# Two blocks in one launch: splits, sums and output pieces at new places, and the up gate scaled by VectorE

## The chip, the cores and the metric

One Trainium2 chip, one of its cores. The metric is the device time of one launch in microseconds; the kernels are compared by the median of their runs. A profile is one execution taken by the hardware profiler.

## The reference

An input x of 256 tokens by 1024 features goes through two blocks, in float32.

```
first block, for each of 2 layers:
  h = rms_norm(x); proj = h @ w_in                      # 1024 -> q, k, v of two attentions, gates
  y_a = dilated_attention(q, k, v with rope) @ w_proj_a
  y_b = stick_breaking_attention(q, k, v) @ w_proj_b
  x = x + (gate_a * y_a + gate_b * y_b) @ w_out
  h = rms_norm(x); a, b = split(h @ w_up)               # 2 x 2816
  x = x + (silu(causal_conv(a)) * b) @ w_down
x = rms_norm(x)
second block, one layer:
  proj = rms_norm(x) @ w_in                             # qkv, z, b, a, lru_x, lru_gate
  o  = gated_delta_rule(silu(conv(qkv)), ...); gdn = rmsnorm(o) * silu(z)
  hr = rg_lru(conv(lru_x), ...);               lru = hr * gelu(lru_gate)
  x = x + concat(gdn, lru) @ w_out
  u = relu(rmsnorm(x) @ w_ff1); x = x + (u * u) @ w_ff2 # 4096 wide
out = rmsnorm(x)
```

## The kernel before

The activations lie transposed (features on the 128 partitions, 256 tokens along the row), 8 chunks wide. Every weight matrix is cut into slabs of up to 128 x 2048 values (two output tiles of 128 features over 8 chunks; 1024 values where there are 4 chunks). Three slabs are in work at a time (SLOTS = 3): SyncE loads slab n into `raw`, ScalarE rounds it to `w_hi` (fp32r), and VectorE, or GpSimd for the slabs listed in POOL_SLABS, writes the rest `raw - w_hi` to `w_lo`. These are the splits (L1280 on ScalarE, L1776 on VectorE, L2500 on GpSimd). Each product of a chunk is then three matmuls, high by high, high by low and low by high (`main_tile`, L671). SyncE loads slab n + 3 when slab n's low half is written. ScalarE splits slab n + 3 when TensorE has ended slab n. Activations are split in the same way: `xg_hi`/`xg_lo`, and for inner results `hid_high` on ScalarE and `hid_low` on VectorE (L1856). The results of a slab go to PSUM, into three banks in turn (RING = 3), two tiles to a bank for most kinds and one for the kinds that are added to x; a tile may begin when the one three banks earlier has been read.

The order on each engine is written out by hand, one program for each, which wait on semaphores. What stands where in an engine's program is all that sets the order.

Up stages of the first block (L941 for TensorE): slabs of kind "fa" (the convolved half) and "fb" (the other half) alternate, 12 in the first part and 10 in the second, of each layer. For an fa slab VectorE multiplies both tiles by the norm (L2047), ScalarE does the last tap, VectorE the two others, ScalarE splits slab n + 3 and applies silu (L1479), and GpSimd multiplies by the norm (L2555). For an fb slab VectorE multiplies the product by that (L2050), ScalarE writes the high half and then splits slab n + 3, VectorE writes the low half (L2066) and then splits slab n + 3. A pair of slabs is one fa and one fb.

Input stage of the second block (L1152, L2341): 13 slabs. Between tiles and in the middle of tiles TensorE does the small matmuls of the delta rule: `first_x` (L1016) turns the first matrices; for levels 1 to 6 `level_ax`, `level_x` and `turn_x` follow; VectorE answers with `level_mask` (L2245) and `level_add` (L2258), ScalarE with `turned_x`. `key_gain` and `matrix_a` (L2150, L2216) make the matrices that first_x turns. `unit_out` (L2323) is the end of the recurrence: four scans, four products, then four low halves at L2395.

Output stage of the second block: 4 slabs "lru" and 4 slabs "gdn", 4 chunks each; `x_add` (L1792) adds each tile to x. After the lru tile 4 TensorE does `spread_out`, from which VectorE makes the gdn half of the input (L2452) and its low halves. Then `x_stage` (L1803) interleaves x_add, the splits and `x_low` (the low half of the next stage's input), and the up stage of 4096 features begins.

## Time and profile before

| | us |
|---|---|
| median of 3 runs | 1090.31 |
| lowest, highest | 1089.19, 1090.49 |
| the profiled execution | 1091.28 |
| its span | 1089.5 |
| TensorE busy (8400 matmuls) | 1068.8 |
| VectorE busy | 705.4 |
| ScalarE busy | 570.8 |
| GpSimd busy | 353.9 |
| mean granted TensorE clock | 0.996 |

Busy time is the union of an engine's instructions as the profiler shows them; an instruction may be drawn overlapping the next one, above all on TensorE. A row of a timeline gives the start and the length in us, the engine, the line of the kernel, the operation, what is written and read, the shapes, how many like it were merged, and in brackets the idle time ahead of it with what ended it.

### The profile page before, as it was taken

The numbers are of one execution on the slowest core, as the hardware profiler recorded it, in microseconds if no ns is written. First come the engines' busy times: TensorE is split into PE (matmuls) and PEld (weight loads), VectorE is DVE, ScalarE is ACT, GpSimd is POOL, SyncE is SP. The second block draws the span as 40 slices with busy tenths as digits, with TensorE's granted clock in tenths as the row PEclk, the third lists the DMA queues.
The fourth block names the chain that finished last, engine by engine and source line by source line (L and its number), as shares of the span: only waits on it lengthen the run. The fifth ranks groups of instructions, "written<-read, shape, count | busy, mean of one in ns | idle before, by whom it ended". The sixth has DMA issues, their size and how long they took to land.

```text
span 1089.5 us, 20040 instructions
## 1 busy us (share of the span) xinstructions
PE 1068.8 (98%) x8400; PEld 1008.4 (93%) x8400; DVE 705.4 (65%) x1164; ACT 570.8 (52%) x788; POOL 353.9 (32%) x223
## 2 busy tenths in 40 slices
PE   8999999999999999999999999999999999999997
PEld 6999998998899899999999989998989999999996
DVE  4752248767677776222877767777877778667663
ACT  5545466554355544545665544466637856344433
POOL 1386675322023128666642201323200034102020
PEclk9999999999999999999999999999999999999999
DMA  7744454454754665344545475446341156564751
GB/s 251 232 162 138 141 180 156 155 184 149 247 173 141 198 219 182 107 148 152 161 157 185 153 229 194 135 143 212 119 154 41 59 176 204 170 212 136 234 184 39
DMA packets 169689, 180.11 MB, mean 165 GB/s; under 512 B 4224, under 2 KB 166400, under 8 KB 169472
## 3 DMA queue, kind: packets, MB, share of 16 engines
q1 hardware_dynamic: 169600, 178.84, 51.0%
q8 instruction: 66, 1.08, 0.4%
q14 instruction: 23, 0.19, 0.1%
HBM read 177.78 MB, written 1.05 MB: 164 GB/s over the span
## 4 chain that ended last, share of the span: by engine, by line
PE 70%; issue 11%; DVE 10%; ACT 5%; POOL 3%; DMA 1%; SPq 0%; DVEq 0%; POOLq 0%; ACTq 0%
PE psum L669 68%; DVE sb_w_lo L1783 3%; ACT sb_w_hi L1278 2%; POOL sb_scratch L2535 1%; POOL sb_scratch L2555 1%; ACT sb_scratch L1278 1%; DVE sb_scratch L1774 1%; PE psum L865 1%; DVE sb_rs L1832 1%; DVE sb_xg_lo L1774 1%; DVE sb_hid_both L1858 1%; DMA sb_scratch<-in_x 1%; DMA sb_raw<-in_w_ff 1%; DVE psum L1774 0%; ACT sb_xg_hi L1278 0%
## 5 line engine op out<-in xcount | busy, mean ns | idle before, releaser
L669 PE MATMUL psum<-sb_xg_hi,sb_w_hi 128*128 128x256 f32 x1640 | 471.1, 287 | 4.8 <-DVE sb_w_lo L1783 2.8
L669 PE MATMUL psum<-sb_xg_lo,sb_w_hi 128*128 128x256 f32 x1640 | 464.3, 283 | 0.0
L669 PE MATMUL psum<-sb_xg_hi,sb_w_lo 128*128 128x256 f32 x1640 | 464.2, 283 | 0.0
L1278 ACT ACTIVATE sb_w_hi<-sb_raw 128x2048 fp32r<-128x2048 f32 (+4 forms) x184 | 316.0, 1722 | 160.0 <-PE psum L669 97.9
L1783 DVE TENSOR_TENSOR sb_w_lo<-sb_raw,sb_w_hi 128x2048 fp32r<-128x2048 f32 (+3 forms) x150 | 304.8, 2037 | 115.6 <-ACT sb_w_hi L1278 115.5
L669 PEld LDWEIGHTS psum<-sb_xg_hi,sb_w_hi 128*128 128x128 f32 x1640 | 313.9, 191 | 10.7 <-issue 5.8
L669 PEld LDWEIGHTS psum<-sb_xg_lo,sb_w_hi 128*128 128x128 f32 x1640 | 314.2, 192 | 0.4
L669 PEld LDWEIGHTS psum<-sb_xg_hi,sb_w_lo 128*128 128x128 f32 x1640 | 314.0, 191 | 0.2
L669 PE MATMUL psum<-sb_hid_both,sb_w_hi 128*128 128x512 f32 (+1 forms) x912 | 281.7, 369 | 2.3 <-DVE sb_hid_both L1858 1.3
L669 PE MATMUL psum<-sb_hid_both,sb_w_lo 128*128 128x256 f32 x784 | 221.0, 282 | 0.0
L669 PEld LDWEIGHTS psum<-sb_hid_both,sb_w_hi 128*128 128x128 f32 x912 | 164.1, 190 | 36.6 <-issue 3.5
L2506 POOL TENSOR_TENSOR sb_w_lo<-sb_raw,sb_w_hi 128x2048 fp32r<-128x2048 f32 (+1 forms) x34 | 154.9, 4562 | 123.2 <-ACT sb_w_hi L1278 111.1
L669 PEld LDWEIGHTS psum<-sb_hid_both,sb_w_lo 128*128 128x128 f32 x784 | 149.2, 190 | 0.0
L2555 POOL TENSOR_TENSOR sb_scratch<-sb_scratch,sb_rs 128x256 f32<-128x256 f32 x44 | 66.2, 1524 | 242.0 <-ACT sb_scratch L1278 242.0
L1278 ACT ACTIVATE sb_hid_both<-sb_scratch 128x256 fp32r<-128x256 f32 x100 | 40.0, 414 | 96.3 <-DVE sb_scratch L2050 62.7
L1278 ACT ACTIVATE sb_scratch<-sb_scratch,sb_params 128x256 f32<-128x256 f32 x76 | 37.8, 554 | 60.3 <-DVE sb_scratch L2047 60.3
L2583 POOL TENSOR_TENSOR sb_scratch<-sb_scratch 128x256 f32<-128x256 f32 x32 | 23.4, 754 | 125.2 <-DVE sb_scratch L1774 125.2
L1858 DVE TENSOR_TENSOR sb_hid_both<-sb_scratch,sb_hid_both 128x256 fp32r<-128x256 f32 x100 | 51.9, 543 | 4.7 <-ACT sb_hid_both L1278 4.1
L1278 ACT ACTIVATE sb_scratch<-psum 128x256 f32<-128x256 f32 (+3 forms) x58 | 24.7, 463 | 49.7 <-PE psum L669 32.2
L1930 DVE CUSTOM_DVE_ANT_0 sb_scratch<-psum,sb_consts 128x512 f32<-128x512 f32 x16 | 10.4, 689 | 61.9 <-PE psum L669 61.9
L669 PE MATMUL psum<-sb_scratch 64*64 64x32 f32 (+6 forms) x728 | 49.2, 262 | 0.4 <-DVE sb_scratch L2251 0.4
L669 PEld LDWEIGHTS psum<-sb_scratch 64*64 64x64 f32 (+3 forms) x728 | 41.6, 152 | 6.2 <-issue 1.7
(168 smaller groups left out, 1036.7 us busy)
## 6 DMA issues: line engine op xcount, KB each, us to landing
sb_raw<-in_w_in SPq DMA_DIRECT2D x52, 1024.0 KB, 5.1
sb_raw<-in_w_up SPq DMA_DIRECT2D x44, 1024.0 KB, 5.1
sb_raw<-in_w_ff SPq DMA_DIRECT2D x21, 1024.0 KB, 5.6
sb_raw<-in_w_down SPq DMA_DIRECT2D x16, 768.0 KB, 4.8
sb_raw<-in_w_down SPq DMA_DIRECT2D x16, 640.0 KB, 4.4
sb_raw<-in_w_out SPq DMA_DIRECT2D x8, 1024.0 KB, 5.1
sb_raw<-in_w_ff SPq DMA_DIRECT2D x8, 768.0 KB, 4.5
sb_raw<-in_w_ff SPq DMA_DIRECT2D x8, 640.0 KB, 4.5
```

The source lines that it names most:

```text
L669: return nc.tensor.matmul(ps, lhsT, rhs, start=start, stop=stop, skip_group_check=True)
L865: mm = nc.tensor.transpose(psum[:, BANK_T + u % 2, i * P:i * P + P], prob_of(u)[:, i * P:i * P + P], C("ident"))
L1278: return nc.scalar.activation(out_, in_, func, **kw)
L1774: return v.scalar_tensor_tensor(out=out_, in0=a, scalar=scalar, in1=b, op0=op0, op1=op1)
L1783: v.tensor_tensor(part(w_lo, s), part(raw, s), part(w_hi, s).bitcast(F32), ALU.subtract)\
L1832: v.tensor_tensor(tmp, guess_, guess_, ALU.mult).then_inc(S["dve_step"], q.one("dve_step"))
L1858: v.tensor_tensor(hid_lo(i), src, hid_hi(i).bitcast(F32), ALU.subtract).then_inc(S["hid_lo"], 1)
L1930: v.tensor_tensor_reduce(prob_of(u), psum[:, BANK_SC + u % 2, :], C(f"dil_mask{units(u)[1]}"), -HEAD ** -0.5, 3e38, ALU.add, ALU.min, dil_ ...
L2506: g.tensor_tensor(part(w_lo, s), part(raw, s), part(w_hi, s).bitcast(F32), ALU.subtract)\
L2535: g.tensor_tensor(parted(tl(qk, r)), parted(tl(qk, r)), by_parity(swap), ALU.add).then_inc(S["q_tile"], 1)
L2555: g.tensor_tensor(tl(s_scaled, i % 4), tl(s_silu, i % 4), RSTD, ALU.mult).then_inc(S["a_scaled"], 1)
L2583: g.tensor_tensor(tl(h32, i % 4), tl(y_conv, i % 4), tl(y_conv, i % 4), ALU.mult)\
```

## The change

- Up stages of the first block: VectorE scales the gate (L2555's product) itself, at the head of each fb slab, and GpSimd no longer does. In all fb slabs but the last of a part, both ScalarE and VectorE split slab n + 3 ahead of the slab's other work and not behind it.
- Input stage of the second block: slab 5's low half is written by GpSimd and no longer by VectorE. first_x for the first half of the tokens stays behind tile 9, the one for the second half moves into the middle of tile 10. level_add(3) moves from slab 7 to slab 6, behind its convolution and ahead of the splits; the split of slab 9 moves behind level_add(4).
- End of the recurrence: scan t, product t - 1 and low half t - 2 alternate, and ScalarE's split stands ahead of the high halves. TensorE takes chunks 0 and 1 of both tiles of the first lru slab, then chunks 2 and 3.
- Output stage: the x_add of the second tile of lru slab 2 comes behind the gdn low halves. In the gdn slabs the split of the first up slab comes one slab sooner, at slab 1, and the low half of tile 3 is no longer held back. TensorE takes chunks 0 to 4 of both tiles of the first up slab, then chunks 5 to 7.

```diff
--- before.py
+++ after.py
@@ -60,7 +60,7 @@
-POOL_SLABS = {(2, "in"): (3, 4), (2, "out", "lru"): (3,), (2, "out", "gdn"): (0,), (2, "up", 0): (2,)}
+POOL_SLABS = {(2, "in"): (3, 4, 5), (2, "out", "lru"): (3,), (2, "out", "gdn"): (0,), (2, "up", 0): (2,)}
 for _l in range(DEPTH):
...
@@ -1013,13 +1013,10 @@
-            def first_x():
-                for b in range(NB):
-                    if q.due("e_xt0", b + 1):
-                        pe.wait_ge(S["e_xt0"], b + 1)
-                    turn_blocks(pair(b)[0], lambda h, half: diagonal(mat(XT, b, h), half)).then_inc(S["d_x0"], 1)
+            def first_x(b):
+                if q.due("e_xt0", b + 1):
+                    pe.wait_ge(S["e_xt0"], b + 1)
+                turn_blocks(pair(b)[0], lambda h, half: diagonal(mat(XT, b, h), half)).then_inc(S["d_x0"], 1)
...
@@ -1151,6 +1148,8 @@
                 def amid(i):
+                    if i == 10:
+                        first_x(1)
                     if i in (12, 15, 18):
...
@@ -1175,7 +1174,7 @@
                     if i == 9:
-                        first_x()
+                        first_x(0)
                     if i == 10:
...
@@ -1239,6 +1238,11 @@
             for s in plan.stages[(2, "out", "lru")]:
+                if s.index == 0:
+                    for chunks in (range(0, 2), range(2, LT)):
+                        for j, t in enumerate(s.tiles):
+                            main_tile(s, t, j, (hid_parts(GH), "hid_lo", GH), hid_base, chunks=chunks)
+                    continue
                 slab_two(s, (hid_parts(GH), "hid_lo", GH), hid_base, lambda i: spread_out() if i == 4 else None)
...
@@ -1252,7 +1256,14 @@
                 for s in plan.stages[(2, "up", half)]:
-                    slab_two(s, xg, xg_base, between)
+                    if half or s.index:
+                        slab_two(s, xg, xg_base, between)
+                        continue
+                    for j, t in enumerate(s.tiles):
+                        main_tile(s, t, j, xg, xg_base, chunks=range(0, KD - 3))
+                    for j, t in enumerate(s.tiles):
+                        main_tile(s, t, j, xg, xg_base, chunks=range(KD - 3, KD))
+                        between(j)
                 if half < LAST:
...
@@ -1456,6 +1467,9 @@
                     for s in plan.stages[(l, "up", half)]:
+                        ends = s.index == n - 1
+                        if s.kind == "fb" and not ends:
+                            split(s.n + SLOTS)
                         for j in range(2):
...
@@ -1477,7 +1491,7 @@
                                 f(tl(s_silu, r), tl(y_conv, r), ACT.Silu).then_inc(S["a_silu"], q.one("a_silu"))
-                        else:
+                        elif ends:
                             split(s.n + SLOTS)
...
@@ -1714,12 +1728,12 @@
                     act.preload_act_table_set(LOGEXP)
+                    split(s.n + SLOTS)
                     for t in range(LT):
...
                     row_guess()
-                    split(s.n + SLOTS)
             for s in plan.stages[(2, "out", "lru")]:
...
@@ -1800,18 +1814,16 @@
-            def x_stage(slabs, gain, ahead=2, held=()):
+            def x_stage(slabs, gain, ahead=2, sooner=False):
...
                         x_add(m, t)
-                        if gain and j and s is slabs[-2] and len(slabs) == 4:
-                            split(s.n - 1 + SLOTS)
-                            for i in held:
-                                x_low(i, gain)
-                        if gain and m and m - 1 not in held:
+                        if gain and j and len(slabs) == 4 and s is slabs[1 if sooner else 2]:
+                            split(slabs[1].n + SLOTS)
+                        if gain and m:
                             x_low(m - 1, gain)
...
@@ -2038,6 +2050,14 @@
                     for s in plan.stages[(l, "up", half)]:
+                        ahead = s.kind == "fb" and s.index < n - 1
+                        if ahead:
+                            split(s.n + SLOTS)
+                        if s.kind == "fb":
+                            for j in range(2):
+                                r = (f0 + s.index // 2 * 2 + j) % 4
+                                dve.wait_ge(S["a_silu"], q.next("a_silu"))
+                                v.tensor_tensor(tl(s_scaled, r), tl(s_silu, r), RSTD, ALU.mult).then_inc(S["a_scaled"], 1)
                         for j, t in enumerate(s.tiles):
...
@@ -2064,7 +2084,8 @@
                                 hid_low(i - f0, tl(h32, r))
-                        split(s.n + SLOTS)
+                        if not ahead:
+                            split(s.n + SLOTS)
                     last = half == len(PARTS1) - 1
...
@@ -2331,12 +2352,18 @@
                 dve.wait_ge(S["dve_step"], q.sent["dve_step"])
-                for t in range(LT):
-                    v.tensor_tensor_scan(tl(l_r, t), l_a[t], tl(l_i, t), 0.0, ALU.mult, ALU.add)\
-                        .then_inc(S["dve_step"], q.one("dve_step"))
-                dve.wait_ge(S["dve_step"], q.sent["dve_step"])
-                for t in range(LT):
-                    stt(tl(l_scan, t), tl(l_scan, t), 0.5, tl(l_r, t), ALU.mult, ALU.mult).then_inc(S["l_h"], q.one("l_h"))
+                scanned = q.sent["dve_step"]
+                for t in range(LT + 2):
+                    if t < LT:
+                        v.tensor_tensor_scan(tl(l_r, t), l_a[t], tl(l_i, t), 0.0, ALU.mult, ALU.add)\
+                            .then_inc(S["dve_step"], q.one("dve_step"))
+                    if 1 <= t <= LT:
+                        dve.wait_ge(S["dve_step"], scanned + t)
+                        stt(tl(l_scan, t - 1), tl(l_scan, t - 1), 0.5, tl(l_r, t - 1), ALU.mult, ALU.mult)\
+                            .then_inc(S["l_h"], q.one("l_h"))
+                    if t >= 2:
+                        dve.wait_ge(S["l_h"], t - 1)
+                        hid_low(GH + t - 2, tl(l_scan, t - 2))
...
@@ -2373,7 +2400,6 @@
                 if n == 7:
-                    level_add(3)
                     attend(1)
...
@@ -2390,9 +2416,6 @@
                     unit_out()
-                    dve.wait_ge(S["l_h"], q.sent["l_h"])
-                    for t in range(LT):
-                        hid_low(GH + t, tl(l_scan, t))
                     row_var()
...
@@ -2414,13 +2437,14 @@
                     convolve(s)
+                    level_add(3)
                     split(slabs[5].n + SLOTS)
-                    split(s.n + SLOTS)
                     continue
...
                     level_add(4)
+                    split(slabs[6].n + SLOTS)
                 if n == 8:
...
@@ -2434,7 +2458,8 @@
                 x_add(2 * n, s.tiles[0])
-                x_add(2 * n + 1, s.tiles[1])
+                if n != 2:
+                    x_add(2 * n + 1, s.tiles[1])
                 if n == 0:
...
@@ -2455,8 +2480,9 @@
                         hid_low(h, tl(z_t, h))
+                    x_add(2 * n + 1, s.tiles[1])
                 split(s.n + SLOTS)
-            x_stage(plan.stages[(2, "out", "gdn")], lambda m: col("norm_mlp", m), held=(3,))
+            x_stage(plan.stages[(2, "out", "gdn")], lambda m: col("norm_mlp", m), sooner=True)
             stats += 2
...
@@ -2546,13 +2572,6 @@
                 split((l, "up", 0))
-                for i in range(FF_TILES):
-                    pool.wait_ge(S["a_silu"], q.next("a_silu"))
-                    if q.due("h_tile", FF_TILES * l + i - 3):
-                        pool.wait_ge(S["h_tile"], FF_TILES * l + i - 3)
-                    if q.due("rstd", 2 * l + 2):
-                        pool.wait_ge(S["rstd"], 2 * l + 2)
-                    g.tensor_tensor(tl(s_scaled, i % 4), tl(s_silu, i % 4), RSTD, ALU.mult).then_inc(S["a_scaled"], 1)
                 add_squares(2 if l == DEPTH - 1 else 1)
...
```

## Rows read from the trace of the kernel before

**Rows 1.** The page: busy time and share of an engine; granted clock in 40 slices.
```profile
PE 1068.8 (98%) x8400; PEld 1008.4 (93%) x8400; DVE 705.4 (65%) x1164; ACT 570.8 (52%) x788; POOL 353.9 (32%) x223
PEclk9999999999999999999999999999999999999999
```

**Rows 2.** Engines by stretch: start:end and length, busy us (instructions) of PE first, PEclk, DMA.
```profile
223.30:235.20 11.90, 11.75 (x96) 11.57 (x96) 8.66 (x13) 6.15 (x8) 3.25 (x2) 1.00 0.55 178
...
297.00:345.00 48.00, 48.00 (x403) 48.00 (x402) 34.91 (x49) 24.77 (x33) 12.96 (x8) 1.00 0.50 162
```

**Rows 3.** Timelines of PE, DVE, POOL and ACT, one pair of up slabs.
```profile
235.28 0.36 PE L669 MATMUL psum<-sb_xg_hi,sb_w_hi 128*128 128x256 f32 x1 [0.20 <-DVE sb_w_lo L1783]
...
223.10 0.75 DVE L2047 TENSOR_TENSOR sb_scratch<-psum,sb_rs 128x256 f32<-128x256 f32 x2
224.19 1.93 DVE L1774 SCALAR_TENSOR_TENSOR sb_scratch<-sb_scratch,sb_params 128x256 f32<-128x256 f32 x4 [0.34 <-ACT sb_scratch L1278]
226.49 2.29 DVE L1783 TENSOR_TENSOR sb_w_lo<-sb_raw,sb_w_hi 128x2048 fp32r<-128x2048 f32 x1 [0.37 <-ACT sb_w_hi L1278]
229.49 0.42 DVE L2050 TENSOR_TENSOR sb_scratch<-psum,sb_scratch 128x256 f32<-128x256 f32 x1 [0.71 <-POOL sb_scratch L2555]
...
232.84 2.29 DVE L1783 TENSOR_TENSOR sb_w_lo<-sb_raw,sb_w_hi 128x2048 fp32r<-128x2048 f32 x1 [1.38 <-ACT sb_w_hi L1278]
235.05 0.75 DVE L2047 TENSOR_TENSOR sb_scratch<-psum,sb_rs 128x256 f32<-128x256 f32 x2
...
226.84 3.25 POOL L2555 TENSOR_TENSOR sb_scratch<-sb_scratch,sb_rs 128x256 f32<-128x256 f32 x2 [8.69 <-ACT sb_scratch L1278]
...
226.36 0.70 ACT L1278 ACTIVATE sb_scratch<-sb_scratch 128x256 f32<-128x256 f32 x2
```

**Rows 4.** Timelines of PE, DVE and ACT, before slab 5 of the second block's input.
```profile
781.31 0.36 PE L669 MATMUL psum<-sb_xg_hi,sb_w_hi 128*128 128x256 f32 x1 [1.61 <-DVE sb_w_lo L1783]
...
778.27 0.69 DVE L2231 TENSOR_TENSOR sb_scratch<-sb_scratch,sb_consts 128x512 f32<-128x512 f32 x1
778.88 2.28 DVE L1783 TENSOR_TENSOR sb_w_lo<-sb_raw,sb_w_hi 128x2048 fp32r<-128x2048 f32 x1
...
770.02 1.91 ACT L1278 ACTIVATE sb_w_hi<-sb_raw 128x2048 fp32r<-128x2048 f32 x1
```

**Rows 5.** Timelines of POOL and DVE, norm ahead of the first up stage.
```profile
193.03 4.92 POOL L2506 TENSOR_TENSOR sb_w_lo<-sb_raw,sb_w_hi 128x2048 fp32r<-128x2048 f32 x1 [4.94 <-ACT sb_w_hi L1278]
...
195.16 3.08 DVE L1832 TENSOR_TENSOR sb_rs<-sb_rs 128x256 f32<-128x256 f32 x1 [1.35 <-ACT sb_rs L1278]
```

**Rows 6.** Timelines of DVE and PE at level 3, and one stretch of all engines.
```profile
807.37 4.48 DVE L1783 TENSOR_TENSOR sb_w_lo<-sb_raw,sb_w_hi 128x2048 fp32r<-128x2048 f32 x2
...
826.43 0.48 DVE L2254 TENSOR_TENSOR sb_scratch<-psum,sb_consts 128x128 f32<-128x128 f32 x2
...
812.11 1.09 PE L669 MATMUL psum<-sb_consts,sb_scratch 64*64 64x64 f32 x30 [1.82 <-DVE sb_scratch L2265]
...
815.00:818.00 3.00, 3.00 (x16) 2.90 (x16) 1.04 (x4) 0.00 (x0) 0.00 (x0) 0.63 0.78 246
```

**Rows 7.** Timelines of DVE and PE, end of the recurrence, and one stretch.
```profile
864.31 2.44 DVE L2335 TENSOR_TENSOR_SCAN sb_scratch<-sb_scratch,sb_sq 128x256 f32<-128x256 f32 x4
...
868.82 0.36 PE L669 MATMUL psum<-sb_hid_both,sb_w_hi 128*128 128x256 f32 x1 [0.88 <-DVE sb_hid_both L1858]
...
878.00:881.00 3.00, 3.00 (x15) 2.67 (x14) 0.00 (x0) 0.00 (x0) 2.23 (x1) 0.61 0.60 175
```

**Rows 8.** Timelines of DVE and PE, gdn output and start of the last up stage.
```profile
894.53 0.74 DVE L1796 TENSOR_TENSOR sb_xt<-sb_xt,psum 128x256 f32<-128x256 f32 x2
895.19 2.28 DVE L1783 TENSOR_TENSOR sb_w_lo<-sb_raw,sb_w_hi 128x2048 fp32r<-128x2048 f32 x1
...
897.57 0.36 PE L669 MATMUL psum<-sb_xg_hi,sb_w_hi 128*128 128x256 f32 x1 [0.88 <-issue]
901.15 0.39 PE L669 MATMUL psum<-sb_xg_hi,sb_w_hi 128*128 128x256 f32 x1 [0.53 <-DVE sb_xg_lo L1774]
```

## The prediction

> **What bounds the kernel now.** I read the page first. TensorE is busy for 1068.8 of 1089.5 us and its clock is full nearly throughout [rows 1], so only its idle stretches, and the pieces with the lower clock, can be won. Next I read what ended TensorE's waits, then the timelines of all engines round each of them. Leaving out start and tail, about 9.8 us of idle time stand between 27 and 902 us, most of it in five kinds of place: the up products of both attention layers (eight stalls of about 0.2 us), 779.7, 810.3, 867.9 and 896 to 901 us. The change touches each. One correction holds for all: a matmul is drawn 0.28 us long while the next one starts 0.12 us later, so a stall costs about 0.16 us more than the idle time shown. The up stage shows it: a stretch of 11.9 us with a stall holds 96 matmuls, while 48 us without one touch 403, 0.12 us each [rows 2]; 96 then need 11.5 us.
>
> The profiled execution took 1091.28 us (span 1089.5 and 1.8 around it); the three timed ones have their median at 1090.31. I sum against the profiled one and take 1.0 off at the end, by that difference.
>
> **Part 1, the gate's scaling in the up stages.** Before, a pair of slabs repeats every 11.94 us on VectorE (223.10 to 235.05, [rows 3]), though TensorE needs only 11.5. So the loop through four engines sets the pace: take the a tiles, ScalarE's tap and silu, GpSimd's scaling, product, high half, ScalarE's split, VectorE's split. The split that ends at 235.13 is the one for which TensorE waits at 235.28 [rows 3]. GpSimd needs 3.25 us for two scalings, because the first runs into VectorE's split of 226.49 to 228.78, and VectorE then waits 0.71 us for the first and a little for the second [rows 3]. VectorE waits 1.38 us more, as ScalarE splits only after both high halves.
>
> After: VectorE's busy time in a pair is 8.8 us by its rows (0.75 + 1.93 + 2.29 + four of 0.42 + 2.29) [rows 3], plus two scalings at 0.42 (its product has the same size): 9.6. ScalarE's second split comes right behind silu, at 227.1 (silu runs from 226.36 for 0.70), done 1.9 later at 229.0, which costs VectorE 0.2 us of wait behind its own split of 228.78. With 0.7 for tap and first split and 0.3 for the high halves the loop takes 10.8 us, under TensorE's 11.5. Behind the new wait for ScalarE's split are queued the scaling, the product and the low halves, and nobody needs those low halves before the down stage. The three stalls in the first up stage of each layer (0.38 each, 11.94 less 11.55) and the one at each down stage's start (0.21 shown, 0.37 in all) go: 6 x 0.38 + 2 x 0.37 = 3.0. The first pair starts late after the norm and may keep 0.1 to 0.2. **I take -2.8 us** (-3.0 to 0).
>
> **Part 2, slab 5 of the third input stage goes to GpSimd.** TensorE idles 1.61 us before slab 5, since VectorE splits it from 778.88, behind the matrices of the delta rule [rows 4]. On GpSimd the split can start when ScalarE's is done, at 771.93 [rows 4], and takes 4.6 us where nothing holds it up (one that VectorE disturbs takes 4.92 [rows 5]), so it is ready at 776.6, well before TensorE's turn at 779.7. But VectorE is in the middle of work with two operands in SBUF. What happens then is in the trace: GpSimd's split of 193.03 to 197.95 overlaps a subtraction-sized product of VectorE that starts at 195.16 and ends at 198.24, 3.08 us instead of 0.41, 0.29 behind GpSimd's end [rows 5]. Four more such pairs in the trace end 0.28 to 0.30 apart, this is the first of its kind at a norm. The key gain (two small operands) and the two matrices take VectorE 5.5 us and end with the addition of 778.27 at 778.96 [rows 4], so the key gain is at 773.4, and VectorE would stand there until 776.6: the matrices are ready at 779.6 and 782.1 instead of 776.5 and 779.0. TensorE, which is there at 778.3 (779.7 less 32 small matmuls), then waits 1.2 us for the first, does half a tile, waits 0.2 for the second (first_x(1) now stands there) and pays some 0.2 for one more change between small and large matmuls. The 1.6 us is only paid elsewhere. Slab 6's split ends about 1.2 us later, at 789.6, just where TensorE needs it. **I take +0.2** (-1.5 if the hold does not bite, +1.0 if more slips).
>
> The Trainium skill, SBUF — State Buffer, "Who interferes with whom", says that a VectorE instruction with two SBUF inputs and a GpSimd instruction that reads SBUF exclude each other for the whole instruction, whoever starts first. By that rule, the trace agrees with its 3.08 us; and were the rule wrong for the 128x8 operands of the key gain, this part would be worth 1.5 us.
>
> **Part 3, level_add(3) ahead of the splits.** At 807.37 VectorE does two splits, 4.48 us, and only then the addition for which TensorE has waited 1.82 us [rows 6]. The products it needs start at about 806.7 and are done by 807.8. After: addition at 807.5 to 808.2, and TensorE's turn at 810.3 finds it done: 1.82 + 0.16 = -1.98. In the profiled execution the clock then falls to the lower level of its two (2.4 and 1.2 GHz) for about 3.4 us: 815 to 818 has a mean of 0.63 [rows 6], and half a tile of 12 matmuls takes 2.9 us against 1.7. That is 1.5 us more, near half of the 3.4. What TensorE did before it fell: 1.82 us idle, then small matmuls. Without the idle time I expect it to stay up: -1.5 (0 to -1.5).
>
> What is late next: slab 9's split (2.29 us) now stands between level_add(4) and slab 7's convolution, behind which come slab 10's split and level_mask(5). The latter ran at 826.43 [rows 6] for 0.48, with TensorE there at 828.1: 1.2 us of room. Counted from level_x(3), level_add(4) ends at +11.2 (TensorE no longer stalled nor slowed before it), then 2.3 + 3.0 + 2.3 us bring level_mask(5)'s first half to +18.8, and TensorE asks at +18.3. **+0.6** (0 to +1.3, as ScalarE's gates of the next logits also hang on that convolution). Part 3 together: -2.9.
>
> **Part 4, the recurrence's output.** Scan, product and low half now alternate, and TensorE takes chunks 0 and 1 of both tiles first. But ScalarE does a split (1.04 us) ahead of the high halves, after slab 12 frees its place at 866.1: first high half at 867.6. VectorE now waits for it before its fourth scan. By [rows 7] a scan takes 0.61 us; a product or low half 0.36, half of the 0.75 that two take in [rows 3]: first low half at 868.1, second at 869.4. TensorE starts 0.7 sooner, stands about 0.9 before chunk 1, and ends the slab at 872.0 against 871.7. **+0.3** (-0.8 to +1.0). The fall of the clock at 878.7 (mean 0.61 in 878 to 881, [rows 7]) comes behind the small products of spread_out, which stay: I count nothing (0 to -1.5).
>
> **Part 5, gdn output and first slab of the last up stage.** Moving x_add(5) behind the low halves lets these start at 878.6 instead of waiting 3.75 us, which brings slab gdn 1's split, and with it the load of up slab 0, about 2 us forward. The split of that slab, 895.19 to 897.47, ended just before TensorE's start at 897.57, after 0.88 us idle; 0.53 more went for a low half at 901.15 [rows 8]. Both go: 0.88 + 0.53 + 0.32 = -1.7. But the split now stands (about 892.7 to 895.0) ahead of x_add(4), which ran at 894.53. With three PSUM banks tile 7 needs that addition, at 895.25, and it now ends at about 895.9: +0.7. **-1.0** (-1.7 to +0.2).
>
> **Sum.** -2.8 + 0.2 - 2.9 + 0.3 - 1.0 = -6.2: profiled 1085.1, median 1084.1. Since each new order can cost a few tenths I have not seen, I say **1084.5**.
>
> **Rivals.** (a) The clock's fall isn't avoided, or comes at one of the new stalls of 0.6 to 1.2 us: 1084.5 + 1.5 = 1086.0. For it: two falls in this trace, one behind only a short stall. (b) The shared hold is milder or the stalls of parts 2 and 5 don't come: up to 1.7 + 0.7 less, near 1082.5. Against: five rows with the same 0.3 us. (c) The up part does nothing, since another link of the loop takes GpSimd's place: 1084.5 + 2.8 = 1087.3. Against: 0.7 us of room. (d) Slower: VectorE becomes the bound of the up stages. It decides when its loop passes 11.55 us; at 12.4 (if both waits of 1.38 for ScalarE's split came twice) 22 pairs cost 0.85 each, 18.7 us in place of the 2.8 won, some of it taken by slack that the stages without stalls have: about 1100. Against: its busy time would be 9.6 of 11.5. (e) The new stalls eat all but a little: 1088 to 1090.
>
> **Chances.** Forecast 0.48, (a) 0.22, (b) 0.14, (c) 0.06, (e) 0.06, (d) 0.04. Range 1081.0 to 1088.3: it takes in (a), (b), (c) and the bounds of parts 2 to 5, and leaves out most of (d) and (e). A difference of 0.2% (2.2 us) is about what a measurement of this kernel can tell: faster than 1088.1 has 0.91, within 0.2% 0.05, slower 0.04.
>
> **What would show it.** In the up stages no TensorE wait for the weights' low half and a pair in 11.5 to 11.6 us of VectorE's timeline. At 773 to 777 one VectorE instruction of about 3 us on the small tile, and TensorE waiting for the identity addition near 778.5. No wait for level_add(3), but one for level_mask(5) near the turn of slab 8. A short wait for the second low half of the recurrence near 868. A wait for x_add(4) before the last gdn tile. The clock's mean in 811 to 820 at 1.00. Wrong would be a VectorE loop over 11.6 us, or a fall of the clock at a new place.

## The result

The changed kernel takes 1080.9 us in the median (1079.6 to 1081.7), the kernel before, run beside it, 1089.9 us: a ratio of 0.9916, 95% interval 0.9899 to 0.9934. That is 9.0 us less, where 5.8 were forecast; the stated range ended at 1081.0, a tenth above the result. The profiled execution of the kernel after took 1080.86 us (span 1079.0). Two executions on record, one of u0_up_undone with 1138.4 us and one of the kernel before with 3633.3 us, lie far outside all others and are left out of every comparison.

The page of the kernel after, beside [rows 1]:

```profile
span 1079.0 us, 20002 instructions
...
PE 1062.2 (98%) x8400; PEld 1005.7 (93%) x8400; DVE 717.8 (67%) x1207; ACT 570.5 (53%) x788; POOL 292.3 (27%) x180
...
PEclk9999999999999999999999999999999999999999
```

GpSimd has lost 61.6 us of work (353.9 to 292.3) and VectorE has gained only 12.4 (705.4 to 717.8). TensorE's busy time fell by 6.6 us although its 8400 matmuls are the same; part of that is clock, part is waits that the page draws as busy time. So I read the gain from where the k-th matmul starts in either trace (both have all 8400): what a matmul starts later than its counterpart, it has lost up to there. Columns: the stretch, in the times of the kernel after; how far after's matmuls have moved against before's within it; my forecast.

| stretch | moved, us | forecast |
| --- | --- | --- |
| first 14 us (start) | +1.3 | none |
| up and down stages, layer 0 / layer 1 | -2.6 / -2.6 | -2.8 for both |
| pace of the out stage's matmuls, layer 1 (531 to 550) | -0.3 | none |
| slab 5 of the third input stage (775) | +0.15 | +0.2 |
| level_add(3) and level_mask(5) (806 to 821) | -3.0 | -2.9 |
| recurrence's output (861 to 870) | -0.1 | +0.3 |
| clock at 871 to 875 (878.7 in before) | -1.5 | 0 |
| gdn output, first up slab (871 to 895) | -1.85 | -1.0 |

They sum to -10.45, -11.8 without the start. (The profiled executions differ by 10.4 us and the medians by 9.0, since the profiled one of before lies 1.4 above its median.) What still makes TensorE wait in the kernel after, by the view of waits (line it is waiting for: us in total, times, longest):

```profile
PE psum L669 <- DVE sb_scratch L2252: 1.5, 2, 1.4
...
PE psum L669 <- DVE sb_xt L1810: 1.3, 1, 1.3
PE psum L669 <- DVE sb_w_lo L1797: 1.0, 3, 0.5
PE psum L669 <- DVE sb_hid_both L1870: 0.9, 2, 0.6
...
PE psum L669 <- DVE sb_scratch L2272: 0.4, 1, 0.4
PE psum L669 <- DVE sb_scratch L2275: 0.3, 1, 0.3
```

The first line is slab 5's hold, the second the wait for x_add(4), the fourth the two low halves of the recurrence, the last level_mask(5): four waits that the forecast had announced at those places. The third line, three waits ahead of 600 us, stands in before as well, and the line for L2272, 0.37 us at level_mask(6), is new and was not announced. The up stages' stalls for the weights' low half are gone.

VectorE's timeline in the up stage of the kernel after (start, length, line, operation; L2060 is the new scaling, L2070 the product, L2067 the taking of the a tiles, L1797 the split):

```profile
222.49 0.75 DVE L2067 TENSOR_TENSOR sb_scratch<-psum,sb_rs 128x256 f32<-128x256 f32 x2
223.58 1.92 DVE L1788 SCALAR_TENSOR_TENSOR sb_scratch<-sb_scratch,sb_params 128x256 f32<-128x256 f32 x4 [0.34 <-ACT sb_scratch L1289]
225.88 4.71 DVE L1797 TENSOR_TENSOR sb_w_lo<-sb_raw,sb_w_hi 128x2048 fp32r<-128x2048 f32 x2 [0.38 <-ACT sb_w_hi L1289]
230.50 0.75 DVE L2060 TENSOR_TENSOR sb_scratch<-sb_scratch,sb_rs 128x256 f32<-128x256 f32 x2
231.17 0.75 DVE L2070 TENSOR_TENSOR sb_scratch<-psum,sb_scratch 128x256 f32<-128x256 f32 x2
...
232.75 0.42 DVE L2067 TENSOR_TENSOR sb_scratch<-psum,sb_rs 128x256 f32<-128x256 f32 x1
```

A pair of slabs now takes VectorE 10.26 us (222.49 to 232.75), against 11.94 before [rows 3] and 10.8 in the forecast: two splits back to back, two waits of 0.34 and 0.38 left. Four pairs in a row take 10.2 to 10.3 us (212.23 to 253.23), less than TensorE's 11.5: VectorE, late behind the norm, catches up.

### The profile page after: what moved, and what is told of

It reads as the page before. It is cut to its first block, busy times and chain, and to the rows that moved or that the text cites. A ratio compares the mean times of both kernels' runs of the same rounds, so it can differ in the third digit from the quotient of the medians.

```text
span 1079.0 us, 20002 instructions
## 1 busy us (share of the span) xinstructions
PE 1062.2 (98%) x8400; PEld 1005.7 (93%) x8400; DVE 717.8 (67%) x1207; ACT 570.5 (53%) x788; POOL 292.3 (27%) x180
## 4 chain that ended last, share of the span: by engine, by line
PE 88%; DVE 6%; ACT 2%; POOL 2%; issue 1%; DMA 1%; SPq 0%; DVEq 0%; POOLq 0%; ACTq 0%
PE psum L669 87%; DVE sb_w_lo L1797 3%; POOL sb_scratch L2561 1%; ACT sb_w_hi L1289 1%; PE psum L865 1%; DMA sb_scratch<-in_x 1%; DVE psum L1788 0%; DVE sb_scratch L1788 0%; POOL sb_rs L2548 0%; POOL sb_scratch L2557 0%; DVE sb_small L2181 0%; PE psum L786 0%; ACT sb_sq L1289 0%; DVE sb_hid_both L1870 0%; DVE sb_xg_lo L1788 0%
## 5 line engine op out<-in xcount | busy, mean ns | idle before, releaser
L1797 DVE TENSOR_TENSOR sb_w_lo<-sb_raw,sb_w_hi 128x2048 fp32r<-128x2048 f32 (+3 forms) x149 | 302.4, 2031 | 114.0 <-ACT sb_w_hi L1289 113.1
L669 PE MATMUL psum<-sb_hid_both,sb_w_hi 128*128 128x512 f32 (+1 forms) x912 | 278.6, 366 | 2.7 <-DVE sb_xt L1810 1.3
L2532 POOL TENSOR_TENSOR sb_w_lo<-sb_raw,sb_w_hi 128x2048 fp32r<-128x2048 f32 (+1 forms) x35 | 159.6, 4563 | 128.7 <-ACT sb_w_hi L1289 116.6
L2548 POOL TENSOR_TENSOR sb_rs<-sb_sq 128x256 f32<-128x256 f32 x7 | 5.5, 794 | 345.4 <-ACT sb_sq L1289 345.4
L1942 DVE CUSTOM_DVE_ANT_0 sb_scratch<-psum,sb_consts 128x512 f32<-128x512 f32 x16 | 10.4, 689 | 61.9 <-PE psum L669 61.9
```

Of the source, the lines that this page charges most:

```text
L669: return nc.tensor.matmul(ps, lhsT, rhs, start=start, stop=stop, skip_group_check=True)
L1797: v.tensor_tensor(part(w_lo, s), part(raw, s), part(w_hi, s).bitcast(F32), ALU.subtract)\
L1942: v.tensor_tensor_reduce(prob_of(u), psum[:, BANK_SC + u % 2, :], C(f"dil_mask{units(u)[1]}"), -HEAD ** -0.5, 3e38, ALU.add, ALU.min, dil_ ...
L2532: g.tensor_tensor(part(w_lo, s), part(raw, s), part(w_hi, s).bitcast(F32), ALU.subtract)\
L2548: g.tensor_tensor(SUMS[n], tl(sq, 2 * n) if m == 1 else SUMS[n], tl(sq, 2 * n + m % 2), ALU.add)\
```

## Experiments

All start from the kernel after and are compared with its trace, matmul by matmul. Executions differ by up to 2.2 us in the first 14 us, where all these kernels are the same, so movements are counted behind the start. Two more slips of 0.3 to 0.35 us, spread evenly over the 512-column matmuls of the out stages (170 to 190 and 531 to 550), are in some executions and not in others, also of the kernel after itself; they are left out. ("Waits" and "stalls" are times in which an engine stands still, "a fall" is a stretch in which TensorE's granted clock is at the lower of its two levels.) Line numbers differ by a few between kernels.

### Which edit of the up stages does it, and what is it worth?

u0_up_undone takes both edits back: the scaling on GpSimd, the splits behind the products.

```
-                        if s.kind == "fb" and not ends:
-                            split(s.n + SLOTS)
...
-                        if ahead:
-                            split(s.n + SLOTS)
...
-                                v.tensor_tensor(tl(s_scaled, r), tl(s_silu, r), RSTD, ALU.mult)
...
+                    g.tensor_tensor(tl(s_scaled, i % 4), tl(s_silu, i % 4), RSTD, ALU.mult)
```

> The kernel after, with the whole up part of the attention layers as it was before (GpSimd scales the gate, both splits behind the products). My forecast priced this part at 2.8 us, which would give 1083.7 us. Theory from comparing the two traces matmul by matmul: it is worth 5.5 us (2.6 in layer 0, 2.9 in layer 1), of which three stalls of 0.36 in each layer and about 1.3 at the start of each down stage, where waits of 0.1 to 0.4 hide under matmuls drawn 0.5 us long; so 1086.4 us. If the 2.7 us of difference come from elsewhere (run to run, the norm before the stage), this run stays near 1083.7.

1087.1 us in the median (ratio to before 0.9968, 0.9954 to 0.9982). In the trace 5.9 us come back in the two layers, of which 0.65 is the pace of the out stages. So this part is worth 5.3 us (5.2 between the traces of before and after), nearly twice my term and near the theory's 5.5. The same trace shows where most of what I missed lies. VectorE at the start of layer 0's down stage, first here, then in the kernel after (L1810 here and L1813 there are the same addition):

```profile
265.69 0.42 DVE L2059 TENSOR_TENSOR sb_scratch<-psum,sb_scratch 128x256 f32<-128x256 f32 x1 [0.20 <-POOL sb_scratch L2569]
...
267.98 3.43 DVE L1794 TENSOR_TENSOR sb_w_lo<-sb_raw,sb_w_hi 128x1536 fp32r<-128x1536 f32 x2 [0.96 <-ACT sb_w_hi L1289]
271.33 0.42 DVE L1810 TENSOR_TENSOR sb_xt<-sb_xt,psum 128x256 f32<-128x256 f32 x1
```

```profile
264.82 1.76 DVE L1797 TENSOR_TENSOR sb_w_lo<-sb_raw,sb_w_hi 128x1536 fp32r<-128x1536 f32 x1 [1.45 <-ACT sb_w_hi L1289]
...
267.48 0.42 DVE L1813 TENSOR_TENSOR sb_xt<-sb_xt,psum 128x256 f32<-128x256 f32 x1
```

TensorE enters the down stage 1.7 us later than in the kernel after, but VectorE's addition comes 3.8 us later: it brings the lag of its loop along. TensorE then stops for low halves, a split and a bank between 266 and 272. Its starts slip by 1.28 us there, though the list of its waits shows only this:

```profile
266.51 0.50 PE L669 MATMUL psum<-sb_hid_both,sb_w_hi 128*128 128x512 f32 x1 [0.23 <-DVE sb_hid_both L1867]
```

A matmul of 512 columns is drawn 0.40 to 0.50 us long while the next one starts 0.24 us later, so waits of up to 0.25 us behind it leave no gap. In before itself the starts slip against after by the same amount, 1.26 us, between 264.3 and 270.9.

u1_splits_early keeps the early splits and gives the scaling back to GpSimd.

```
-                                v.tensor_tensor(tl(s_scaled, r), tl(s_silu, r), RSTD, ALU.mult)
+                    g.tensor_tensor(tl(s_scaled, i % 4), tl(s_silu, i % 4), RSTD, ALU.mult)
```

> The kernel after, with the splits early as in after but GpSimd scaling the gate as before. Theory: the place of the splits breaks the loop through four engines, not the engine of the scaling. VectorE's pair of slabs is then 10.26 less 0.75 for the scalings it no longer does, plus two GpSimd scalings of 0.65 that stand between and behind its two splits: about 10.8 us, under TensorE's 11.5. So no stall in the up stages, and 1081.2 us (1080.9 to 1081.7). Rival: two splits in a row keep GpSimd from its operands until the second has ended, both scalings then come one by one, the pair is 12 us or more, and the time is 1085 us or above.

1080.5 us (0.4 below the theory's range), and in the trace within 0.1 us of the kernel after. Its loop (L2062 is the taking of the a tiles, from 221.39 to 231.71):

```profile
221.39 0.75 DVE L2062 TENSOR_TENSOR sb_scratch<-psum,sb_rs 128x256 f32<-128x256 f32 x2
...
224.78 5.05 DVE L1797 TENSOR_TENSOR sb_w_lo<-sb_raw,sb_w_hi 128x2048 fp32r<-128x2048 f32 x2 [0.37 <-ACT sb_w_hi L1289]
...
230.46 0.42 DVE L2065 TENSOR_TENSOR sb_scratch<-psum,sb_scratch 128x256 f32<-128x256 f32 x1 [0.30 <-POOL sb_scratch L2576]
...
231.71 0.75 DVE L2062 TENSOR_TENSOR sb_scratch<-psum,sb_rs 128x256 f32<-128x256 f32 x2
```

10.32 us a pair. The theory held: GpSimd's scalings fall beside the splits and cost VectorE 0.34 within these (5.05 for 4.71) and 0.30 of wait, a little less than the 0.75 of doing them itself.

u2_scale_vector keeps the scaling on VectorE and puts the splits back behind the products.

```
-                        if s.kind == "fb" and not ends:
-                            split(s.n + SLOTS)
...
-                        elif ends:
+                        else:
                             split(s.n + SLOTS)
...
-                        if ahead:
-                            split(s.n + SLOTS)
...
-                        if not ahead:
-                            split(s.n + SLOTS)
+                        split(s.n + SLOTS)
```

(The first two pieces are ScalarE's, the others VectorE's.)

> The kernel after, with VectorE scaling the gate but the splits behind the products as before. Theory: the loop keeps its length but for the waits for GpSimd: scalings at 228.8, products to 230.3, ScalarE's split to 232.5, VectorE's to 234.8, a pair of about 11.65 us against the 11.5 of TensorE. Stalls of 0.15 a pair stay (0.9 us in all), and most of what is lost at the start of the down stages (2.4 us): 1084.2 us (1083 to 1085). Rival: it is the engine of the scaling that matters, and the time is that of the kernel after, 1080.9 us.

1081.3 us; the trace shows no wait for a split in the up stages, and its starts don't slip against the kernel after there or at the head of the down stages. (It ends 0.1 us before that of the kernel after, by slips of pace alone: +0.7 in the out stages, and -0.4 in each layer's down stage, 272 to 296 and 632 to 658, which no other of the 14 traces has.) My theory (1084.2) missed; the rival gave the time, but not the reason, as u1_splits_early had the scaling on GpSimd and the same time. The loop runs from 223.98 to 235.50:

```profile
223.98 0.75 DVE L2061 TENSOR_TENSOR sb_scratch<-psum,sb_rs 128x256 f32<-128x256 f32 x2
...
229.57 0.76 DVE L2054 TENSOR_TENSOR sb_scratch<-sb_scratch,sb_rs 128x256 f32<-128x256 f32 x2
...
233.29 2.29 DVE L1794 TENSOR_TENSOR sb_w_lo<-sb_raw,sb_w_hi 128x2048 fp32r<-128x2048 f32 x1 [1.37 <-ACT sb_w_hi L1289]
...
235.50 0.75 DVE L2061 TENSOR_TENSOR sb_scratch<-psum,sb_rs 128x256 f32<-128x256 f32 x2
```

That is 11.52 us a pair, just TensorE's own 11.52 (96 matmuls of 0.12). In this loop VectorE waits only for ScalarE and ScalarE only for VectorE, so 11.52 is the loop's own length. The steps of the estimate were right to 0.13 us, but the answer turned on 0.15: a loop just under TensorE's pace costs nothing, one 0.4 above it (11.94) costs 5.3 us over the kernel. The two edits are alternatives: either one is worth the whole, and the second adds nothing that these runs can tell (1080.5 and 1081.3 us beside 1080.9).

### Slab 5 and the hold by GpSimd

s5_slab5_vector leaves slab 5's split to VectorE, behind the matrices of the delta rule.

```
-POOL_SLABS = {(2, "in"): (3, 4, 5), ...
+POOL_SLABS = {(2, "in"): (3, 4), ...
```

> The kernel after, with slab 5 of the third input stage split by VectorE again. Theory: GpSimd's split of 4.6 us holds a VectorE instruction of 128x8 for 3.4 us (0.17 expected without it), the matrices come 3.2 us late, and TensorE waits 1.36 and 0.19 for them; without it those two waits are gone and the wait of about 1.6 before slab 5 is back: 1080.9 less 0.15, within 0.3 of the kernel after. In the trace the instruction of 128x8 at about 769 takes 0.2 us. Rival: the early split in itself helps what follows (slab 6 and 7 are ready sooner), and the time is 1 us or more above the kernel after.

1083.8 us in the median, and 2.1 us more than the kernel after at this place of the trace; my expectation (within 0.3) missed. The hold is what I said it was. GpSimd and VectorE in the kernel after:

```profile
767.83 4.62 POOL L2532 TENSOR_TENSOR sb_w_lo<-sb_raw,sb_w_hi 128x2048 fp32r<-128x2048 f32 x1 [4.78 <-ACT sb_w_hi L1289]
...
769.06 3.42 DVE L2181 TENSOR_SCALAR sb_small<-sb_small 128x8 f32<-128x8 f32 x1
```

and in s5_slab5_vector, with what TensorE then meets:

```profile
767.38 0.17 DVE L2181 TENSOR_SCALAR sb_small<-sb_small 128x8 f32<-128x8 f32 x1
...
775.45 0.55 PE L669 MATMUL psum<-sb_xg_hi,sb_w_hi 128*128 128x256 f32 x1 [2.29 <-DVE sb_w_lo L1797]
```

Engines by stretch there (start:end, length, busy us of PE, PEld, DVE, ACT, POOL, granted clock, DMA share, GB/s):

```profile
775.50:778.30 2.80, 2.80 (x14) 2.58 (x14) 2.73 (x9) 0.00 (x0) 1.88 (x2) 0.50 0.68 169
```

Held 3.42 us against 0.17. Without the hold the 1.36 and 0.19 us of waits go, but TensorE now has only one first_x ahead of slab 5 (the change moved the other into the slab), so the wait for the split is 2.29, not the 1.61 of [rows 4], and the clock then falls to the lower level, 1.2 us more. I had counted the undone edit as the old kernel and forgotten its neighbour.

s5b_slab5_before_gain puts VectorE's split between the eight sums of the keys' squares and the key gain.

```
-POOL_SLABS = {(2, "in"): (3, 4, 5), ...
+POOL_SLABS = {(2, "in"): (3, 4), ...
...
+                split(plan.stages[(2, "in")][2].n + SLOTS)
                 dve.wait_ge(S["e_ksum"], q.sent["e_ksum"])
                 v.tensor_scalar(k_norm2, k_norm, EPS2, None, ALU.add)...
...
-                    split(slabs[2].n + SLOTS)
```

> The kernel after, with slab 5 split by VectorE right behind the eight sums of the keys' squares and ahead of the key gain, so that GpSimd touches nothing there. Theory: the hold is the whole price of slab 5 on GpSimd. Split 769.1 to 771.4 in the times of the kernel after, key gain and first matrix ready at about 774.5 where TensorE asks at 774.24, second at 776.9 where it asks at 776.9: of its 1.36 + 0.19 us of waits 0.3 stay, 1.3 us less, 1079.6 us. Rival: the matrices are held by something else than GpSimd (the bracket at 769.06 shows a long instruction, not who holds it), and they come 2.3 us later still: 1083 us.

At its place as expected: 1.17 us less (TensorE waits 0.18 and 0.18 there), so the hold is the price of slab 5 on GpSimd. But the median is 1081.7 us (expected: 1079.6), nothing below the kernel after. The trace gives the 1.17 back, and more, at 887:

```profile
881.83 1.91 ACT L1289 ACTIVATE sb_w_hi<-sb_raw 128x2048 fp32r<-128x2048 f32 x1 [1.42 <-DMA sb_raw<-in_w_ff]
...
887.31 0.55 PE L669 MATMUL psum<-sb_hid_both,sb_w_hi 128*128 128x256 f32 x2 [2.09 <-DVE sb_xt L1810]
```

```profile
887.30:890.00 2.70, 2.69 (x13) 2.69 (x14) 2.36 (x5) 2.44 (x6) 2.03 (x4) 0.56 0.97 288
```

The second fence is the stretch behind it (granted clock 0.56). In the kernel after:

```profile
881.81 1.92 ACT L1289 ACTIVATE sb_w_hi<-sb_raw 128x2048 fp32r<-128x2048 f32 x1 [0.60 <-DMA sb_raw<-in_w_ff]
...
883.76 2.29 DVE L1797 TENSOR_TENSOR sb_w_lo<-sb_raw,sb_w_hi 128x2048 fp32r<-128x2048 f32 x1 [0.24 <-ACT sb_w_hi L1289]
...
887.30 0.51 PE L669 MATMUL psum<-sb_hid_both,sb_w_hi 128*128 128x256 f32 x2 [1.27 <-DVE sb_xt L1810]
```

The load of the last up stage's first slab lands at 881.8 in both. ScalarE's split, VectorE's split and x_add(4) follow in a row, and TensorE goes on at 887.3 in both. In this execution what was won upstream is waited for here (2.09 where 1.27 was), and behind the longer wait the clock falls as well, 1.5 us.

That is not because the load stays where it is. Its issue by SyncE, and the time from issue to landing (last number, us), in the kernel after:

```profile
876.10 0.37 SPq L632 DMA_DIRECT2D sb_raw<-in_w_ff  x1
sb_raw<-in_w_ff SPq DMA_DIRECT2D x1, 1024.0 KB, 5.7
```

and here:

```profile
875.28 0.37 SPq L632 DMA_DIRECT2D sb_raw<-in_w_ff  x1
sb_raw<-in_w_ff SPq DMA_DIRECT2D x1, 1024.0 KB, 6.5
```

The issue comes 0.82 us sooner, as much as TensorE is ahead there, and the load takes 0.87 longer. This load takes 5.4 to 5.9 us in 11 of the 14 traces, and 6.4 to 6.5 in this one, in m1_masks_and_halves and in u0_up_undone, which changes nothing near it; what makes it long is open. With 5.7 us most of the gain would have been kept, by these numbers as an estimate, and one of the four executions may show that: 1078.3 us, against 1081.5 to 1082.4 of the others.

### Part 3 undone

l3_add3_late puts level_add(3) behind both splits and slab 9's split into its old place.

```
                 if n == 7:
+                    level_add(3)
...
                     convolve(s)
-                    level_add(3)
                     split(slabs[5].n + SLOTS)
+                    split(s.n + SLOTS)
                     continue
...
                     level_add(4)
-                    split(slabs[6].n + SLOTS)
```

> The kernel after, with level_add(3) back behind both splits and slab 9's split back in its old place. Theory: against the trace of the kernel after, TensorE's wait of 1.8 us before level_x(3) is back (+2.0), the wait of 0.34 for level_mask(5) goes (-0.4), and the clock falls behind the wait (+1.5): +3.1 in the trace, 1084.0 us. Rival, by what the run with the up part undone has shown at 878 (same matmuls, same waits in front, the clock fell in one execution and not in another): the fall is a matter of the execution and not of this wait, so it can be missing here; then +1.6, 1082.5 us.

1086.9 us in the median, where 1084.0 was expected, with single executions from 1081.7 to 1087.8. In the trace: +1.88 for the wait, -0.41 for level_mask(5), both as expected, and +3.1 for the clock, twice the +1.5 expected (a further fall of 1.5 at 876 is dealt with below):

```profile
807.29 0.91 PE L669 MATMUL psum<-sb_consts,sb_scratch 64*64 64x64 f32 x24 [1.82 <-DVE sb_scratch L2286]
```

```profile
808.40:815.10 6.70, 6.70 (x55) 6.28 (x54) 3.05 (x8) 0.57 (x3) 0.00 (x0) 0.51 0.67 215
```

The low clock lasted 6.8 us here (808.1 to 814.9, the fence shows most of it) and 3.4 in before, behind the same wait of 1.82. Five of the seven executions took 1086.1 to 1087.8 us at a mean granted clock of 0.992 to 0.994, the other two 1081.7 and 1082.2 at 0.998. So the price of this one order differs by some 5 us between executions.

### Part 5 undone

f5_gdn_undone gives the lru output, the gdn output and TensorE's first up slab their old order.

```
-                if n != 2:
-                    x_add(2 * n + 1, s.tiles[1])
+                x_add(2 * n + 1, s.tiles[1])
-            x_stage(plan.stages[(2, "out", "gdn")], ..., sooner=True)
+            x_stage(plan.stages[(2, "out", "gdn")], ..., held=(3,))
```

> The kernel after, with the edits of the gdn output and of the last up stage's first slab undone (x_add(5) of the lru output ahead of the low halves, the split behind x_add(5), low half 3 held, the slab in two halves of the old cut). Forecast: this part was worth 1.0, 1081.9 us. Theory from the traces: it was worth 1.85 against the trace of before, though with a wait of 1.39 that the load explains; so 1082.7 us.

1083.3 us, nearer to the theory's 1082.7 than to the forecast's 1081.9, and 2.2 us more in the trace. Beside the stalls of [rows 8] waits came back that [rows 8] don't show: starts slip by 0.67 us at the first gdn tile (877.4; 0.27 at that tile in before) and by 0.27 at 891.3 (as in before).

### What else can be had

p1_split_after_add4 moves VectorE's split behind x_add(4) and leaves all else.

```
-                        if gain and j and len(slabs) == 4 and s is slabs[1 if sooner else 2]:
+                        if gain and j == (not sooner) and len(slabs) == 4 and s is slabs[2]:
```

> The kernel after, with VectorE's split of the last up stage's first slab one place further back, behind x_add(4). Theory: TensorE's wait of 1.27 before gdn tile 7 (1.39 in all) is for that addition, which stood behind the split; the addition needs 0.4 us and its operand is there at 883.6, so the wait goes and none takes its place, since x_add(5) comes at 887.1 and its bank is asked for at 887.5: -1.4, 1079.5 us. Rival: x_add(5) becomes late in its stead and -0.5 to 0 is left.

Missed, 1083.0 us (expected: 1079.5). The wait of 1.27 went (-1.43), and the next addition became late:

```profile
884.49 0.66 DVE L1788 SCALAR_TENSOR_TENSOR sb_xg_lo<-sb_xt,sb_params,sb_xg_hi 128x256 fp32r<-128x256 f32 x1 [1.13 <-ACT sb_xg_hi L1289]
...
885.41 2.50 DVE L1797 TENSOR_TENSOR sb_w_lo<-sb_raw,sb_w_hi 128x2048 fp32r<-128x2048 f32 x1
...
889.15 0.39 PE L669 MATMUL psum<-sb_xg_hi,sb_w_hi 128*128 128x256 f32 x1 [1.86 <-DVE sb_xt L1810]
```

VectorE waits 1.13 us for a high half that ScalarE makes only after its own split, then splits, and x_add(5) comes at 888.7 where TensorE asked at 887.3. I had left out ScalarE's order. Behind the wait of 1.86 the clock falls too; in the trace the edit costs 2.1 us in all.

m1_masks_and_halves moves four steps at two places.

```
                     level_mask(5)
+                    split(slabs[7].n + SLOTS)
                 if n == 9:
                     level_mask(6)
+                    split(slabs[8].n + SLOTS)
...
-                    split(s.n + SLOTS)
                     for t in range(LT):
                         ...
                         hid_high(GH + t, tl(l_scan, t))
+                    split(s.n + SLOTS)
```

> The kernel after with two edits at different places of the trace. First, the splits behind slabs 7 and 8 of the third input stage go behind level_mask(5) and level_mask(6): the waits of 0.34 and 0.37 at 821.1 and 830.8 go, -0.9. Second, ScalarE takes the high halves of the recurrence ahead of its split: the waits of 0.31 and 0.57 for the low halves at 861.3 and 862.4 go, -1.1, unless the split of the next slab, now 0.8 to 1.4 us later on ScalarE, is then late for TensorE at about 865 (+0.5). Together -2.0 (-1.3 to -2.2): 1078.9 us. Rival: the first-come order holds, another wait takes the place of each, and nothing is gained.

1080.3 us, where 1078.9 was expected. Before 887 the trace shows 0.5 us less at the two masks (0.85 won, 0.37 given back at once by a later addition) and 1.0 at the recurrence, then 2.2 are lost at x_add(4), again by a wait of 1.99 and a clock of 0.52 behind it. TensorE was 1.4 us ahead of the kernel after there, and so was the issue of the load of w_ff; but the load took 6.4 us for 5.7 and landed only 0.7 sooner. One of the four executions took 1076.8 us.

q2_adds_ahead puts both additions where the load can't hold them.

```
-                        if gain and j and len(slabs) == 4 and s is slabs[1 if sooner else 2]:
+                        if gain and m == (4 if sooner else 5) and len(slabs) == 4:
                             split(slabs[1].n + SLOTS)
+                        if sooner and m in (3, 4):
+                            continue
+                        if sooner and m == 5:
+                            x_low(2, gain)
+                            x_low(3, gain)
```

> The kernel after, with VectorE's order in the gdn output changed: x_add(4) ahead of the split of the first up slab, x_add(5) right behind it, and the low halves 2 and 3 after that. Theory from the four traces in hand: the moment is set by the load of w_ff (it lands at 881.8 whatever TensorE has gained before), ScalarE's split of it (to 883.7) and VectorE's (2.3 us); the two additions need no high half and wait only by their place. x_add(4) then at 883.9, split 884.3 to 886.6, x_add(5) to 887.0, ahead of 887.5: TensorE's wait of 1.27 goes whole, -1.4, 1079.5 us. Rival: the low halves 2 and 3, which now end at 887.9, stop TensorE in the first up slab, and half or more is given back.

1080.8 us: -1.43 at 887 as expected, no wait for the low halves, and +1.0 at the second up slab, whose split by ScalarE (from 890.28) stands behind the squares and high halves of the additions that have moved:

```profile
890.28 3.70 ACT L1289 ACTIVATE sb_w_hi<-sb_raw 128x2048 fp32r<-128x2048 f32 x2
...
892.22 2.29 DVE L1797 TENSOR_TENSOR sb_w_lo<-sb_raw,sb_w_hi 128x2048 fp32r<-128x2048 f32 x1 [1.32 <-ACT sb_w_hi L1289]
...
894.65 0.36 PE L669 MATMUL psum<-sb_xg_hi,sb_w_hi 128*128 128x256 f32 x1 [0.85 <-DVE sb_w_lo L1797]
```

So the theory's wait went, the time it named (1079.5) missed, and neither it nor the rival named what took its place.

best2 has the edits of s5b_slab5_before_gain, m1_masks_and_halves and q2_adds_ahead together, as printed above.

> The kernel after with all that gained in place: slab 5's split by VectorE ahead of the key gain, the splits behind level_mask(5) and (6), the high halves ahead of ScalarE's split at the recurrence, and the additions ahead of the split in the gdn output. Summed singly: -1.2, -0.5, -0.4, -1.0, -1.4 = -4.5. Theory: the last stretch is bound by the load of w_ff, which does not move with TensorE, so that TensorE asks for the first up slab at 884.4 and its split ends at about 886: 1.0 to 1.7 of it are given back, -2.8 to -3.5 in all, 1077.4 to 1078.1 us, and 1.5 more in executions in which the clock falls behind that wait. Rival: it adds up to -4.5, 1076.4 us.

after_again is the kernel after, unchanged.

> The kernel after, unchanged, several times. Theory: two things differ between executions of one kernel, whatever the change: how long the clock stays low in the first 14 us (up to 2.1 us of the time), and whether it falls for 3.4 us (1.5 us of the time) behind a wait or the small matmuls at 870 to 890. Then the times lie at 1079 to 1080 and at 1081 to 1083, lower clock with longer time, and the median of five rounds is 1081.0 (1080.3 to 1082.0).

best2: 1078.0 us (1077.2 to 1079.3, ratio to before 0.9895, 0.9881 to 0.9909); after_again: 1081.6 us (1080.7 to 1082.0, 0.9926). They ran on the same chip together, so best2 is some 3.7 us faster than the kernel after. Of the theory for after_again the median came within its range, and the three longer times have the lower clock (0.997 for 0.998); no execution lay at 1079 to 1080, so two groups of times are not shown. In the trace 4.1 us are gained at the places of the edits, 1.0 is given back at the second up slab (a wait of 0.84 for its split), and 1.5 more where the clock fell in that execution. The theory's time (1077.4 to 1078.1) held, the rival's (all adds up, 1076.4) falls; but the reason was wrong. The load of the first slab took 5.4 us here and was issued and landed sooner along with TensorE; ScalarE's split behind it waited for TensorE and not for the load. The wait is at the second slab.

### The clock

All traces have the eight small matmuls of spread_out behind lru tile 4. These are the stretches of 3.4 us behind them in the kernel after and in u0_up_undone (the third value from the end is the granted clock):

```profile
871.80:875.20 3.40, 3.40 (x31) 3.40 (x30) 3.37 (x10) 2.36 (x5) 1.52 (x1) 1.00 0.66 194
```

```profile
877.80:881.20 3.40, 3.40 (x19) 3.40 (x18) 3.25 (x10) 2.48 (x5) 1.49 (x1) 0.52 0.67 207
```

TensorE's work ahead of them is the same down to the waits: 0.31 and 0.57 us in both, 10 us earlier. The clock stayed at 2.4 GHz in one execution and fell to 1.2 in the other. Of the 14 profiled executions (before, after, twelve experiments) it fell there in four: before, u0_up_undone, l3_add3_late and best2. Each fall cost 1.5 us. In these profiles it also fell behind each of the six waits of 1.8 to 2.3 us: 1.82 in before and in l3_add3_late, 2.29 in s5, 2.09 in s5b, 1.86 in p1, 1.99 in m1. It fell neither behind the waits of 1.3 to 1.4 us at 775.6 (in ten traces) and 887.3 (in seven) nor behind the 1.61 of [rows 4].

The timed executions without a profile say that the long waits don't always bring it. Of 31 of the kernel before, 12 have a mean granted clock of 0.999. That is at most 3.3 us at the lower level in 1089 us, less than one fall, though the order that makes the wait of 1.82 is in all of them. One execution each of s5b (1078.3 us) and m1 (1076.8 us) has 0.999 as well, and they are the shortest of their kernels. (The figure is not always telling: one execution of u2 has 0.947 at an ordinary 1081.8 us.) What decides it in one execution and not in the next is not shown.

## Why the prediction was right or wrong

**Part 1, the size was wrong (5.2 measured, 5.3 by undoing; forecast 2.8).** The mechanism held: a loop through four engines longer than TensorE's 11.5 us, brought under it. The term "the one at each down stage's start (0.21 shown, 0.37 in all)" was mis-sized: it measured 1.26 in layer 0 and 1.28 in layer 1. I took the one gap that the timeline draws and added 0.16, which comes from matmuls of 256 columns; the down stage's have 512, and more waits lie hidden under them, at 265, 268 and 270, all from VectorE's lag. A loop that is too slow also leaves its lag to the next stage; I had ended the account where the loop ends. The six stalls in the up stages measured 0.44 each for 0.38, and the 0.2 that I took off for the first pair was not lost. VectorE's busy time in a pair was as forecast (9.5 measured, 10.26 less its two waits, for 9.6), though the terms as I wrote them add up to 8.9 and 9.8, not 8.8 and 9.6: two multiplications drawn together take 0.75, not twice 0.42. My forecast treated the edits as one, and the experiments show that either would have done.

**Part 2, right (+0.15 for +0.2).** The held instruction, the two waits (1.36 and 0.19 for 1.2 and 0.2) and their places came as written, and without GpSimd's split the hold is gone. One detail differs: the hold caught the addition on 128x8 ahead of the key gain, which has one operand in SBUF, where I let it start at the first with two. The Trainium skill, SBUF — State Buffer, "Who interferes with whom", lists tensor_scalar among the operations that can use both ports, where their operands allow it, and then contend as well; this trace agrees, with 3.42 us against 0.17.

**Part 3, right between these two traces (-3.0 for -2.9).** Wait, clock and the new wait for level_mask(5) (0.41 for 0.6) came as said. But half of it, the clock's 1.5, I read from one execution, and that it fits is in part luck: in 12 of 31 executions of before the granted clock leaves no room for a fall to avoid, and undoing this part cost 4.6 in one execution, by a fall twice as long, and 6.0 in the median.

**Part 4, near (-0.1 for +0.3).** Two waits of 0.31 and 0.57 stand where I had 0.9; the start came earlier than I thought.

**The clock at 878.7: counted at nothing, differs by 1.5 between the two traces, and is not the change's.** The reason in the forecast (the small products stay) was right: the fall comes and goes with the execution. It is one reason why the trace's -11.8 is larger than the medians' -9.0: the profile of before has two falls and lies 1.4 us above its median. The start makes 1.3 of the difference.

**Part 5, the size was wrong (-1.85, 2.2 by undoing; forecast -1.0).** The stalls taken away were worth 3.2 and not 1.7: the two that I counted measured 1.9, and 1.3 lay in waits of 0.1 to 0.4 that are hidden here too (0.37 at the first gdn tile, 0.30 and 0.38 around 899.3 and 900.0 in before). The new one was 1.4 and not 0.7. The step "the split now stands (about 892.7 to 895.0) ahead of x_add(4)" was right in order and wrong in its clock, in two places. Without its wait TensorE would have asked at 885.9 (887.30 less 1.43); the split ended at 886.05, 0.2 behind that, where I had it end 0.25 ahead: I let it follow from VectorE's order, while it follows from the load (ScalarE waits 0.60 us for it). And the low half between the split and the addition took 0.95 us, where such a one takes 0.48 at 882.71, while GpSimd added squares beside it:

```profile
884.10 3.40 POOL L2548 TENSOR_TENSOR sb_rs<-sb_rs,sb_sq 128x256 f32<-128x256 f32 x2 [3.36 <-ACT sb_sq L1289]
...
885.97 0.95 DVE L1788 SCALAR_TENSOR_TENSOR sb_xg_lo<-sb_xt,sb_params,sb_xg_hi 128x256 fp32r<-128x256 f32 x1
```

That GpSimd held it is read from its likeness to [rows 5]; no run took GpSimd away there.

Both wrong sizes have one sign. 2.4 us more in part 1 and 0.85 in part 5 are 3.3 of the 3.6 us between 1084.5 and 1080.9; that the rest is small owes something to chance, since it sets profiled against timed executions. Rival (b) was nearest in time (1082.5), but for its reason nothing speaks: the hold and the new stalls all came. The 0.4 us that I added for "a few tenths I have not seen" had no row behind it.
